# Last mixer of a two-block network: gate projection between the attention slots, forget sums added to the scores by TensorE

## The reference, cut to what matters

```
def mixer_c(h, w_in, forget_bias, q_norm_g, k_norm_g, w_out):
    proj = h @ w_in
    q, k, v, gate, f_logit = split_cols(proj, [D_FOX, D_FOX, D_FOX, D_FOX, N_FOX_HEADS])
    q = rms_norm_2(q.reshape(b, t, N_FOX_HEADS, HEAD_DIM_2), q_norm_g) * (HEAD_DIM_2 ** -0.5)
    k = rms_norm_2(k.reshape(b, t, N_FOX_HEADS, HEAD_DIM_2), k_norm_g)
    log_f = jax.nn.log_sigmoid((f_logit + forget_bias).astype(f32))
    cum = jnp.transpose(jnp.cumsum(log_f, axis=1), (0, 2, 1))
    ...
        s = jnp.einsum('bqhd,bkhd->bhqk', q[:, q0:k_end], k[:, :k_end])
        s = s + cum[:, :, q0:k_end, None] - cum[:, :, None, :k_end]
        prob = jax.nn.softmax(jnp.where(mask, s, -jnp.inf), axis=-1)
        outs.append(jnp.einsum('bhqk,bkhd->bqhd', prob.astype(v.dtype), v[:, :k_end]))
    ...
    o = o * jax.nn.sigmoid(gate)
    return o @ w_out
```

## Time and profile before

| | us |
|---|---|
| median of 3 runs | 2083.54 |
| lowest and highest | 2080.19, 2083.65 |
| the profiled execution, its own time | 2078.96 |
| its span, first to last instruction | 2077.1 |
| PE busy in it | 1968.3 (95%) |
| DVE busy | 1181.6 (57%) |
| ACT busy | 870.7 (42%) |
| POOL busy | 60.3 (3%) |
| mean granted TensorE clock | 0.959 |

### The profile page before, as it was taken

One profiled execution on the slowest core, in us unless ns is written; L12 is line 12 of the kernel. 1 busy time (PEld: TensorE's weight loads), 2 busy tenths in 40 slices (PEclk: granted clock), 3 DMA queues, 4 the chain that ended last, 5 costly groups with the idle time before them and its releaser, 6 DMA issues.

```text
span 2077.1 us, 23954 instructions
## 1 busy us (share of the span) xinstructions
PE 1968.3 (95%) x9946; PEld 1647.4 (79%) x9946; DVE 1181.6 (57%) x1397; ACT 870.7 (42%) x1089; POOL 60.3 (3%) x138
## 2 busy tenths in 40 slices
PE   6999999799999997999998979999999899999998
PEld 6987768678888886888888967888788788667887
DVE  4314353478888896554358834555545459455454
ACT  4313330267767774443221153444444345324443
POOL 0020000000000000000000000000000000210000
PEclk9989999899999999999998999999999989679999
DMA  8332223469898995545230005555555344007551
GB/s 341 140 120 102 95 88 142 168 236 371 329 354 330 345 358 208 182 183 182 102 122 21 1 1 223 183 182 186 199 183 183 142 162 144 19 1 272 182 182 41
DMA packets 51226, 363.74 MB, mean 175 GB/s; under 512 B 5680, under 2 KB 5808, under 8 KB 8496
## 3 DMA queue, kind: packets, MB, share of 16 engines
q1 hardware_dynamic: 50976, 360.13, 46.8%
q10 hardware_dynamic: 144, 2.10, 0.3%
HBM read 361.15 MB, written 1.05 MB: 174 GB/s over the span
## 4 chain that ended last, share of the span: by engine, by line
PE 88%; DVE 6%; ACT 3%; issue 1%; DMA 0%; POOL 0%; SPq 0%; POOLq 0%; DVEq 0%; ACTq 0%
PE bank L2041 8%; PE bank L2418 8%; PE bank L2420 7%; PE bank L2419 7%; PE bank L1987 7%; PE bank L2253 4%; PE bank L2445 4%; PE bank L2443 4%; PE bank L2444 4%; PE bank L2314 3%; PE bank L2316 3%; PE bank L2315 3%; PE bank L2243 3%; PE bank L2329 2%; PE bank L2331 2%; PE bank L2330 2%
## 5 line engine op out<-in xcount | busy, mean ns | idle before, releaser
L1220 DVE TENSOR_TENSOR w_a<-ring,w_a 128x2048 fp32r<-128x2048 f32 x221 | 504.5, 2290 | 303.4 <-ACT w_a L771 303.0
L771 ACT ACTIVATE w_a<-ring 128x2048 fp32r<-128x2048 f32 x221 | 420.6, 1912 | 162.7 <-PE bank L2445 90.7
L2418 PE MATMUL bank<-w_a,h 128*128 128x512 f32 x536 | 214.4, 400 | 11.1 <-DVE h L1275 5.6
L2420 PE MATMUL bank<-w_a,h 128*128 128x512 f32 x536 | 210.2, 392 | 0.0
L2419 PE MATMUL bank<-w_a,h 128*128 128x512 f32 x536 | 209.8, 391 | 0.0
L2041 PE MATMUL bank<-H,ring 128*128 128x256 f32 x800 | 182.7, 385 | 0.0
L1220 DVE TENSOR_TENSOR w_b<-ring,w_b 128x2048 fp32r<-128x2048 f32 x62 | 142.0, 2291 | 66.2 <-ACT w_b L771 65.6
L2041 PEld LDWEIGHTS bank<-H,ring 128*128 128x128 f32 x800 | 151.3, 192 | 26.0 <-issue 5.8
L1987 PE MATMUL bank<-h,w_a 128*128 128x256 f32 x1152 | 144.9, 288 | 7.0 <-DVE h L1275 7.0
L1987 PEld LDWEIGHTS bank<-h,w_a 128*128 128x128 f32 x1152 | 141.4, 194 | 11.1 <-DVE h L1275 7.4
L771 ACT ACTIVATE w_b<-ring 128x2048 fp32r<-128x2048 f32 x62 | 118.7, 1914 | 45.7 <-PE bank L2445 25.7
(11 more groups left out here) (455 smaller groups left out, 3292.5 us busy)
## 6 DMA issues: line engine op xcount, KB each, us to landing
ring<-in_stream SPq DMA_DIRECT2D x330, 1024.0 KB, 4.9
G<-in_gains SPq DMA_DIRECT2D x15, 512.0 KB, 5.8
arena<-in_cmp_w ACTq DMA_DIRECT2D x1, 2048.0 KB, 7.9
sm<-in_small SPq DMA_DIRECT2D x1, 1582.0 KB, 12.9
con<-in_consts SPq DMA_DIRECT2D x1, 1384.0 KB, 17.7
X<-in_x SPq DMA_DIRECT2D x2, 512.0 KB, 3.9
out_x<-X SPq DMA_DIRECT2D x2, 512.0 KB, 2.6
sm<-in_small SPq DMA_DIRECT2D x1, 666.5 KB, 22.7
```

The costliest lines, as they stand in the source:

```text
L771: act.activation(w_slot(unit)[:, 0, :], ring[:, unit % RING, :], ACT.Copy).then_inc(S("w_hi"), 1)
L1220: dve.tensor_tensor(w_slot(unit)[:, 1, :], ring[:, unit % RING, :], w_slot(unit)[:, 0, :].bitcast(FP32), ALU.subtract).then_inc(S("w_lo"), 1)
L2418: pe.matmul(bank[4 + t][:, :], x_hi, w[0][:, k, :], start=first, stop=False)
L2420: ins = pe.matmul(bank[4 + t][:, :], x_lo, w[0][:, k, :], start=False, stop=end)
```

## The change

The gate units are no longer computed in one run. Each is cut into four quarters of 12 matmuls (`gate_quarter`): two quarters run before hs7, one after each of the slots 0 to 13. ACT evacuates a gate unit after the slots 2, 6, 10 and 14. The last two units are split later: unit 14 by ACT before slot 0 and by DVE after slot 1, unit 15 by ACT after slot 2 and by DVE after slot 3.

The forget logits are computed right after c1 and no longer after hs7, and their chain on DVE and ACT is cut into three pieces between the head norms (`forget_1` to `forget_3`). The spreading matmuls, ACT's eight copies and POOL's 32 additions are gone. Instead, in each slot, PE adds the head's sums onto its scores: behind each of the two score matmuls a second one with the same number of columns accumulates into the same part of the bank, with the identity column as weights ("pick"). DVE then adds the constant mask alone. DVE's head_norm(7) moves behind slot 1; slot n waits for the head norm of its own q and k (5 + n // 4). The buffers of the probabilities move into a dead constant area, `sm1`.

```diff
@@ -722,15 +719,6 @@
 
             for name in ("ffn1", "ffn2", "c"):
                 post_power(name)
-            for h in range(N_FOX):
-                b = h % 2
-                pool.wait_ge(S("cb_free"), h // 2 + 1)
-                if h >= 2:
-                    pool.wait_ge(S("fsc_free"), h - 1)
-                m = C("mask3")
-                pool.tensor_tensor(f_mc[:, b, 0:P], m[:, 0:P], f_cum[:, h, 0:P], ALU.add)
-                pool.tensor_tensor(f_mc[:, b, P:3 * P], m[:, P:3 * P], f_cum[:, h, :], ALU.add)\
-                    .then_inc(S("mc"), 1)
             for name in ("ffn3", "end"):
                 post_power(name)
@@ -1162,21 +1150,14 @@
                 evac(f"c{n}", fq[:, 2 * n:2 * n + 2, :], ACT.Copy)
                 if n:
                     head_norm(n - 1)
-            head_norm(7)
-            for n in range(4):
-                split_ahead("c", 12 + n, C_SPLIT)
-
-                if n == 0:
+                if n == 3:
                     act.wait_ge(S("f_dve"), AT["f_abs"])
                     act.activation(fe[0:N_FOX, :], fa[0:N_FOX, :], ACT.Exp, scale=-1.0).then_inc(S("f_act"), 1)
-                if n == 1:
+                if n == 4:
                     act.wait_ge(S("f_dve"), AT["f_one"])
                     act.activation(fl[0:N_FOX, :], fa[0:N_FOX, :], ACT.Ln).then_inc(S("f_act"), 1)
-                evac(f"c{12 + n}", f_gate[:, 2 * n:2 * n + 2, :], ACT.Tanh, scale=0.5)
-            for n in range(8):
-                act.wait_ge(S("cb_full"), n + 1)
-                act.activation(f_cum[:, 2 * n:2 * n + 2, :], tiles(bank[n % 4][:, :], 2), ACT.Copy)\
-                   .then_inc(S("cb_free"), 1)
+            head_norm(7)
+            split("c", 14)
 
             def fox_slot(n):
                 if n < N_FOX:
@@ -1197,6 +1178,10 @@
 
             for n in range(N_FOX + 3):
                 fox_slot(n)
+                if n == 2:
+                    split("c", 15)
+                if n % 4 == 2 and n < N_FOX:
+                    evac(f"c{12 + n // 4}", f_gate[:, n // 2 - 1:n // 2 + 1, :], ACT.Tanh, scale=0.5)
             act.wait_ge(S("fo_free"), KD)
             post_sums("ffn3")
             gated("ffn3")
@@ -1902,41 +1887,55 @@
-            for n in range(2, C_SPLIT - 1):
+            for n in range(2, 14):
                 split("c", n)
-                if 0 <= n - 7 < 8:
+                if n == 7:
+                    forget_1()
+                if n >= 7:
                     head_norm(n - 7)
...
+                if n == 9:
+                    forget_2()
+                if n == 11:
+                    forget_3()
...
-                    dve.wait_ge(S("mc"), n + 1)
                     if n >= 2:
                         dve.wait_ge(S("fexp_done"), 2 * (n - 1))
-                    dve.tensor_tensor(fat_s[:, b, :], bank[b][:, 0:384], f_mc[:, b, :], ALU.add).then_inc(S("fsc_free"), 1)
+                    dve.tensor_tensor(fat_s[:, b, :], bank[b][:, 0:384], C("mask3"), ALU.add).then_inc(S("fsc_free"), 1)
@@ -1962,6 +1961,11 @@
 
             for n in range(N_FOX + 3):
                 fox_slot(n)
+                if n == 1:
+                    split("c", 14)
+                    head_norm(7)
+                if n == 3:
+                    split("c", 15)
             norms("ffn3")
             gated("ffn3")
             norms("end")
@@ -2699,36 +2703,41 @@
                 split_channels(group_begin(f"c{n}"), "c", 4 + n)
                 if n == 1:
                     pe.wait_ge(S("h_32"), H32["c"] + 4)
+                    ps = side_begin("f")
+                    w_f = P2("w_f").rearrange("p (k n) -> p k n", k=KD)
+                    project(ps[0:N_FOX, 0:T], lambda k: w_f[:, k, :]).then_inc(S("side_full"), 1)
                 if n:
                     head_sums(f"hs{n - 1}", f_sq[:, (n - 1) % 2, :], "f_sq", n)
+
+            def gate_quarter(j):
+
+                u, c, late = j // 4, j % 4 // 2, j % 2
+                ps = group_begin(f"c{12 + u}") if j % 4 == 0 else bank[5 + GI[f"c{12 + u}"] % 2]
+                w = split_ready("c", 12 + u)
+                for n in range(12 * late, 12 * late + 12):
+                    wp, x = ((0, h_hi), (1, h_hi), (0, h_lo))[n // KD]
+                    ins = pe.matmul(ps[:, c * T:(c + 1) * T], w[wp][:, n % KD, c * P:(c + 1) * P], x[:, n % KD, :],
+                                    start=(n == 0), stop=(n == 3 * KD - 1))
+                if j % 4 == 3:
+                    ins.then_inc(S("unit_used"), 1)
+
+            gate_quarter(0)
+            gate_quarter(1)
             head_sums("hs7", f_sq[:, 1, :], "f_sq", 8)
-            ps = side_begin("f")
-            w_f = P2("w_f").rearrange("p (k n) -> p k n", k=KD)
-            project(ps[0:N_FOX, 0:T], lambda k: w_f[:, k, :]).then_inc(S("side_full"), 1)
-            for n in range(12, 16):
-                split_channels(group_begin(f"c{n}"), "c", n)
             pe.wait_ge(S("f_cum"), 1)
-            for n in range(8):
-                ps = bank[n % 4]
-                if n >= 4:
-                    pe.wait_ge(S("cb_free"), n - 3)
-                for c in range(2):
-                    h = 2 * n + c
-                    pick = C("ident")[0:N_FOX, h:h + 1].to_broadcast([N_FOX, P])
-                    ins = pe.matmul(ps[:, c * T:(c + 1) * T], pick, fc[0:N_FOX, :], start=True, stop=True)
-                ins.then_inc(S("cb_full"), 1)
-            pe.wait_ge(S("hn_done"), 8)
             pe.wait_ge(S("proj_free"), GI["c11"] + 1)
-            pe.wait_ge(S("cb_free"), 8)
 
             def fox_slot(n):
                 if n < N_FOX:
                     h = slice(HD * (n % 2), HD * (n % 2) + HD)
                     if n >= 2:
                         pe.wait_ge(S("fsc_free"), n - 1)
+                    pe.wait_ge(S("hn_done"), 5 + n // 4)
+                    pick = C("ident")[0:N_FOX, n:n + 1].to_broadcast([N_FOX, P])
                     for t in range(TT):
-                        ins = pe.matmul(bank[n % 2][:, P * t:P * t + P + P * t], fq[h, n // 2, t * P:(t + 1) * P],
-                                        fq[h, KD + n // 2, 0:P * (t + 1)], start=True, stop=True)
+                        ps = bank[n % 2][:, P * t:P * t + P + P * t]
+                        pe.matmul(ps, fq[h, n // 2, t * P:(t + 1) * P], fq[h, KD + n // 2, 0:P * (t + 1)], start=True, stop=False)
+                        ins = pe.matmul(ps, pick, fc[0:N_FOX, 0:P * (t + 1)], start=False, stop=True)
                     ins.then_inc(S("fsc_full"), 1)
                 if 2 <= n < N_FOX + 2:
                     b = n % 2
@@ -2752,6 +2761,8 @@
 
             for n in range(N_FOX + 3):
                 fox_slot(n)
+                if n < 14:
+                    gate_quarter(n + 2)
             pe.wait_ge(S("fo_free"), KD)
             square("c_out", f_o, "ffn3")
             gated("ffn3", "end")
```

More of the change, by code:

```diff
@@ L41 @@
 ARENA = 26368
-SIDES_2 = ["gu0", "gu1", "kk0", "kk1", "bo0", "bo1", "conv", "ln1", "ln2"] + [f"hs{n}" for n in range(8)] + ["f"]
+SIDES_2 = ["gu0", "gu1", "kk0", "kk1", "bo0", "bo1", "conv", "ln1", "ln2"] + ["f"] + [f"hs{n}" for n in range(8)]
 SCALE = HD ** -0.5
@@ L550, in build @@
                 "ffn2": ("ffn1", "half"), "c": ("ffn2", "half"), "ffn3": ("c_out", "whole"), "end": ("ffn3", "half")}
-        SIDE_BEFORE = {"moe": "po1", "ffn1": "ln2", "c": "ln2", "ffn3": "f"}
+        SIDE_BEFORE = {"moe": "po1", "ffn1": "ln2", "c": "ln2", "ffn3": "hs7"}
         BY_TILE = ("ab", "c")
@@ L1903, in head_norm, with forget_1 @@
                                          tiles(f_rs[:, n % 2, :], 2), ALU.mult, ALU.mult).then_inc(S("hn_done"), 1)
-            for n in range(2, C_SPLIT - 1):
+            s = slice(0, N_FOX)
+            def forget_1():
+                dve.wait_ge(S("side_full"), SI["f"] + 1)
+                dve.tensor_scalar(fz[s, :], bank[7][s, 0:T], P2("fb")[s, :], None, ALU.add).then_inc(S("side_free"), 1)
+                dve.wait_ge(S("side_free"), SI["f"] + 1)
+                link(dve.tensor_scalar(fa[s, :], fz[s, :], -1.0, None, ALU.mult))
+                dve.tensor_tensor(fa[s, :], fa[s, :], fz[s, :], ALU.max).then_inc(S("f_dve"), 1)
+                link(dve.tensor_scalar(fm[s, :], fz[s, :], -1.0, 0.0, ALU.mult, ALU.max))
@@ new lines, in forget_2, with forget_3 @@
+            def forget_2():
+                dve.wait_ge(S("f_act"), AT["f_exp"])
+                dve.tensor_scalar(fa[s, :], fe[s, :], 1.0, None, ALU.add).then_inc(S("f_dve"), 1)
+            def forget_3():
+                dve.wait_ge(S("f_dve"), AT["f_one"])
+                link(dve.tensor_scalar(fz[s, :], fa[s, :], -1.0, None, ALU.add))
+                link(dve.tensor_scalar(fc[s, :], fz[s, :], 0.0, None, ALU.is_equal))
+                link(dve.tensor_tensor(fz[s, :], fz[s, :], fc[s, :], ALU.add))
+                link(dve.reciprocal(fz[s, :], fz[s, :]))
+                dve.wait_ge(S("f_act"), AT["f_log"])
+                link(dve.tensor_tensor(fz[s, :], fl[s, :], fz[s, :], ALU.mult))
```

(28 more changed lines are left out.)

13 lines of the change are left out of this document (1 added, 12 removed).

## The result

| | before | after |
|---|---|---|
| median, first set of runs | 2083.2 (4 runs) | 2068.6 (4 runs, 2068.5 to 2072.8) |
| ratio, 95% interval | | 0.9943 [0.9924, 0.9962] |
| the profiled execution; its span | 2078.96; 2077.1 | 2068.54; 2066.6 |
| PE, DVE busy | 1968.3, 1181.6 | 1955.6, 1174.9 |
| mean granted clock | 0.959 | 0.975 |

The change makes the kernel faster, by 0.6% in this set and by 0.4% (0.9959 [0.9944, 0.9975]) when it was timed again beside the experiments. The ratios are those on record with their 95% intervals; they lie up to 0.13% from the quotient of the two medians. The forecast was 2071.

The account below looks back on a forecast made before the run. PE alone was taken to bound the last mixer's slots, at 1.2 GHz. Output projection starting at 1837 instead of 1850.35, less 1, gains 12.3 us: 2066.5 profiled, 2071 as median; own range 2067 to 2075, wider range 2062 to 2079.

Parts of the forecast that it names:

- PE and DVE up to the first slots: Ahead of slot 0: forget logits delay PE by 3.63 us, spreading's 11.5 us goes; DVE has hardly any slack.
- The slots on DVE: Slots 0 and 1 take 4.40 us, then unit 14 and head_norm(7) 6.26, so PE waits for head 1 until 1774.8.
- The slots on PE: Scores 0.85, picks 0.85, transposes 0.48, values 0.79, quarter 1.45: 4.42 us a slot, set by PE; ten slots 44.2.
- rival 2: Dear picks in the slots: shape changes or weight loads make a slot 4.97 us, ten slots 5.5 more, 2077; chance 0.13.
- The clock: Pauses in slots 2 and 3 and the last slots: 8 us at 1.2 GHz in all, costing 4 us.
- slow start of the output projection: Behind the slots: the first stretch of the output projection may still be slow, 1 us.
- The sum: Output projection's start moves from 1850.35 to 1837, less 1: 12.3 us gained; profiled 2066.5, plus 4.6 to the median, 2071.
- Overlap: In odd heads' slots picks run beside scores and cost nothing: 4.3 us less, 2067, or 2063 with full clock; chance 0.22.
- Slower: Clock stays at 1.2 GHz in the slots: 8.4 us a slot, ten slots add 40 us, 2111; chance 0.07.
- No change: DVE's stretch before slot 2 grows by 12 us, so nothing is gained; chance 0.05.

Follow-up runs that it names:

- late_dve: Changed kernel with DVE's low parts of units 14 and 15 and head_norm(7) put behind slots 3, 5 and 7: 2068.41 us, 0.9942 of before.
- pick64: Changed kernel with each pick given the tile shape and rows of its head's scores (64 rows, 48 of them zero): 2064.18 us, 0.9928 of before.
- picks_only: Kernel before with only the spreading replaced by picks, gate units still in one run ahead of the slots: 2095.62 us, 1.0071 of before.
- quarters_only: Changed kernel with the spreading of before, ACT's copies and POOL's additions in place of the picks: 2061.87 us, 0.9920 of before.
- pick64_late: pick64 with DVE's head_norm(6), unit 14, unit 15 and head_norm(7) put behind slots 2, 4, 7 and 9: 2056.02 us, 0.9877 of before.
- woven2: quarters_only with spreading placed between quarters and hs7, unit 14 and head_norm(7) on DVE before slot 0, quarters 4 to 15 in slots 0 to 11: 2057.29 us, 0.9891 of before.
- woven3: woven2 with slots 4 and 9 instead of 12 and 13 left without a quarter: 2057.00 us, 0.9885 of before.

## Why the prediction was right, and where it was not

The number held, 2071 against 2068.6 and 2072.8, and so did the mechanism: the quarters hold the clock, and PE sets the slots. One term of the sum was mis-sized, and that the number is so near is partly luck. By its steps:

- **PE and DVE up to the first slots: right.** hs6 ends at 1750.6 (forecast 1750.2), the forget chain at 1749.4 (1749.0), quarter 0 waits 1.17 us (1.0), DVE reaches slot 0 at 1761.8 (1761.5).
- **The slots on DVE: right in kind.** The wait for the low part and head_norm(7) is there. It ends 0.9 us earlier than forecast (1773.86 against 1774.8), since slots 0 and 1 take 3.47 us and not 4.40, and a later slot 2.16 and not 2.66. late_dve shows that this order of DVE is all of the wait.
- **The slots on PE: mis-sized.** I priced a slot at 4.42 us; it is 4.97. Picks and scores together take 2.08 us where I had 1.70. I had twice the scores' 0.85, of which 0.20 is beyond the columns; but the four matmuls alternate, and each pays that 0.20. The quarter takes 1.62 where I had 1.45 from a long run of them; that the change of shape around it is the reason is likely, but no run takes it apart. Over ten slots that is 5.5 us. It is the slot of rival 2 to the hundredth, though not by its cause: I had it from dear weights for the pick, and pick64 shows that it is the changes of shape, 0.19 us each, on the scores' side too.
- **The clock: right.** Full clock from 1780 to 1836, two dips, at the wait at head 1 and at the end, where I had put them, though I had two pauses of 2 us for the one of 4.36. The first cost 2.1 us (4.97 for three rows and a quarter that take 2.89 at full clock), the end 0.9 beyond the 6.6 us of before (1833.93 to 1841.39); I had allowed 4 for all. My 1 us for a slow start of the output projection before and not after was wrong: it takes 20.99 both times.
- **The sum.** The output projection should have moved from 1850.35 to 1837, and less 1 that was 12.3 us; it moved to 1841.39, 8.96. The 4.4 us between are, up to rounding, the slots' 5.5, less 0.9 of DVE's, less 1 of the clock's, plus 0.9 from the same mis-sized rows outside the ten slots: 0.2 in the rest of slot 3, 0.3 in slot 14 and 0.4 in the scores of slot 15, whose full-clock rows take 2.89, 3.34 and 2.08 us. Behind the output projection the run was 1.5 us shorter, which I had not forecast. The profiled execution should have taken 2066.5 (2078.96 less 12.3 is 2066.7) and took 2068.54. The 4.6 us that I then added, the distance of one profiled execution from its median, were no property of the change: the next median, 2068.6, lies on its profiled execution. So the sum was 2 us too low and with the addition 2.5 too high; that both are so near is luck, as the errors of the terms cancel in part.
- **The rivals.** Overlap: no, odd and even slots are alike, 4.97, and scores and picks start one behind the other; whether the shared bank or the change of shape keeps them apart, no run shows. Slower: picks_only shows it, a clock of 0.50 through the slots and slots of 6.04 us. I gave this 7%; what stands between the change and it is where the quarters lie. No change: no.

What stays open is what exactly makes the clock fall. A pause is not needed: picks_only lost it 5.8 us into slots of narrow matmuls, quarters_only 5.5 us and the kernel before 2.6 us into the spreading, all with PE busy. A pause does not suffice either: pick64_late's of 2.02, 0.76 and 1.08 us left it at 1.00, but one of 0.73 us behind the woven spreading was followed by 0.50 in woven2 and woven3, and the changed kernel lost it 2.2 us into the wait of 4.36. The runs show that a dense quarter in nearly every slot holds the clock; how little would do, they do not.

## What to carry to other kernels

A stage of small matmuls with PE busy all the time can run at 1.2 GHz for tens of microseconds; dense work that has to be done anyway belongs between them, not ahead of them. Narrow matmuls that join others should take the others' tile shape, with zero rows if need be, as each change of shape cost PE some 0.2 us here, at 2.4 GHz. Where a change has two halves, time each alone: here one gained 14.8 us and the other gave 6.2 back. And where executions differ far ahead of the change, compare the length of the stage and not the whole, but do not build on a difference of less than 2 us between two stages read once each.

## What the runs showed of the hardware that I had not expected

DVE's instruction on two columns that negates the maxima (L1943 before, L1942 after) takes 0.63 us in the median beside POOL's additions and 0.17 without them. Duration min/median/max in ns, of before and then of after:

```profile
L1943 DVE TENSOR_SCALAR tiny<-tiny x16: 170/632/647, 1791.3 to 1845.1; 128x2 f32<-128x2 f32 x16
```

```profile
L1942 DVE TENSOR_SCALAR tiny<-tiny x16: 168/170/170, 1763.1 to 1835.3; 128x2 f32<-128x2 f32 x16
```

In quarters_only and woven2, where POOL adds again, it is 0.63 again. That is 0.46 of the 0.50 us by which DVE's slot was shorter than I forecast. The Trainium skill ("GPSIMD Engine Reference", 1. Specifications) says that GpSimd shares its SBUF interfaces with VectorE, with contention for VectorE's instructions in a 2-port perf mode or with two SBUF inputs. The trace agrees for this instruction as far as that it is long only beside POOL; which mode it ran in, no view shows. Its neighbours, the reductions, are as long with POOL as without (0.29 and 0.41 us).
